# The last four input slabs of a hybrid mixer as plain float32 products

## The chip, the cores and the metric

The kernel runs on one core of one Trainium2 chip. The time is device microseconds (us) of one execution, and the measure is the median of several executions. The core has a matrix engine (TensorE, PE in the profile), a vector engine (VectorE, DVE), a scalar engine (ScalarE, ACT), GpSimd (POOL) and SyncE (SP), which here only issues the DMAs that fetch weights.

## The reference

The program is a stack of two small transformer blocks for 256 tokens of width 1024, all in float32. The stage that changes is the input projection of the "even mixer" of the second block:

```python
def even_mixer(h, w_in, w_out, dw_w, dw_b, ln_g, ln_b):
    proj = h @ w_in                                   # (256 x 1024) @ (1024 x 2560)
    q, k, v, u, gate = jnp.split(proj, [512, 1024, 1536, 2048], axis=-1)
    a_out = merge_heads(stick_breaking_attention(     # 8 heads of 64
        split_heads(q, 8), split_heads(k, 8), split_heads(v, 8)))
    c = u * jax.nn.sigmoid(gate)
    c = causal_depthwise_conv(c, dw_w, dw_b)          # 31 taps, 512 channels
    c = jax.nn.silu(layer_norm(c, ln_g, ln_b))
    return jnp.concatenate([a_out, c], axis=-1) @ w_out
```

## The kernel before

**Weights come in slabs.** A slab is 1 MB of a weight matrix (for the input projection 256 output columns), which SyncE's queue fetches into one of four slots `raw[0..3]`. ScalarE then writes the high part of each number to `w_hi` (`high_one`, L587), and VectorE (`low_one`, L1257) or GpSimd (`low_one`, L509) writes the rest, `raw - w_hi`, to `w_lo`. The activations are kept in the same way, in `x_hi` and `x_lo`, the two parts of `x_pair`. Both parts have the type float32r. The product of a slab is then three matmuls instead of one (`three`, L1906 to L1908): high by high, high by low, low by high.

```python
pe.matmul(out_ap, a_hi, b_hi, start=start, stop=False, skip_group_check=True)
pe.matmul(out_ap, a_hi, b_lo, start=False, stop=False, skip_group_check=True)
return pe.matmul(out_ap, a_lo, b_hi, start=False, stop=stop, skip_group_check=True)
```

A slot may be fetched anew when `slab_ready` has counted its low part, since from then on nobody reads `raw`.

**The stage.** The hybrid mixer has ten input slabs. Two wide ones give v; then come the list `HYB_IN`: slab 6 (u, half 0), 8 (gate, half 0), 0 (q, half 0), 2 (k, half 0), and then the four in question: 7 (u, half 1) in slot 0, 9 (gate, half 1) in slot 1, 1 (q, half 1) in slot 2, 3 (k, half 1) in slot 3. Each of these goes through `slab_into`, which makes 2 x 8 x 3 = 48 matmuls of 128 by 128 weights with 256 columns.

**The order is written out by hand on each engine.** TensorE puts the four slabs between the steps of the attention of heads 0 to 3:

```python
heads(stick_logits, 0); slab_into(4, 0)
heads(stick_logits, 1); slab_into(5, 1)
heads(stick_rest, 0);   slab_into(6, 2)
... wait: banks of slabs 0 and 1 are read out ...
heads(stick_values, 0); heads(stick_rest, 1); slab_into(7, 3)
```

`all_copied()` follows, which waits until ScalarE has read the last bank out (L617), then the logits of heads 4 to 7, warming matmuls on zeros (`keep_warm`, L2000), the rest of these heads, and `project_out`, the product with w_out. The logits of a head (L2388 to L2391), its `stick_rest` (L2399 to L2401) and its `stick_values` (L2410 to L2412) are matmuls of plain float32 already.

VectorE runs the depthwise convolution one tap at a time (`convolve(n)` is n taps, L1773). Between them stand its part of the attention, `bounds` (L1779) and `softplus` (L1787), the low parts of slabs, and `gated_half` (L1753), the product u x sigmoid(gate) that feeds half of the convolution. How many taps stand at each place is a constant.

## Time and profile before

| what | value |
|---|---|
| median of 3 runs | 1682.43 us (1682.34 to 1683.7) |
| the profiled execution | 1682.74 us |
| its span, first to last instruction | 1680.7 us |
| TensorE busy / weight loads | 97% / 84% of the span |
| VectorE busy | 71% |
| ScalarE busy | 51% |
| GpSimd busy | 7% |
| granted TensorE clock, mean | 0.997 of full speed |
| input projection of the hybrid mixer and its attention | from about 868 us to about 966 us |

The profiled execution is 2.04 us longer than its span, which is what lies around the first and the last instruction. A matmul's end is modelled in the profile, and matmuls overlap, so what one costs in a stream is read from the distance between two starts, not from its duration.

### The profile page before, as it was taken

Reading aid. Unit: us, or ns where it says so; the run is one execution under the profiler, and the core shown is the slowest. Engines: PE = TensorE matmul, PEld = TensorE weight load, DVE = VectorE, ACT = ScalarE, POOL = GpSimd, SP = SyncE. Lnnn points to the kernel's source line nnn. Section 1 sums busy time; section 2 is a strip of 40 time slices with the busy share of each in tenths; the row PEclk is TensorE's granted clock in tenths of the full one; section 3 lists DMA queues with packets and bytes.
Section 4 is the critical chain, followed back from the end, with each engine's and each line's share of the span. In section 5 each row is a group of like instructions: output and inputs, shape, how many; then the busy total and the mean of one; then the engine's idle time right before and its main releaser. Section 6 shows DMA issues by size and latency. Waiting matters only on the chain. (4 is left out here: it accounts for less than half of the span.)

```text
span 1680.7 us, 24860 instructions
## 1 busy us (share of the span) xinstructions
PE 1635.6 (97%) x9423; PEld 1415.3 (84%) x9432; DVE 1193.1 (71%) x1765; ACT 862.4 (51%) x1212; POOL 115.7 (7%) x36
## 2 busy tenths in 40 slices
PE   8999999989999999999999999999999999999998
PEld 7988888879788887888889778888888888888887
DVE  2896778777668788566679976667666675676665
ACT  6323655572665556544466373446544465364443
POOL 6351000012600000000010000000000000000000
PEclk9999999999999999999999999999999999999999
DMA  8623466755245556455644235555555653345552
GB/s 284 207 76 101 141 213 192 222 145 164 66 149 175 200 175 201 163 196 179 225 144 170 80 128 182 194 184 197 178 187 196 204 200 115 125 138 186 189 195 80
DMA packets 211035, 283.35 MB, mean 169 GB/s; under 512 B 13196, under 2 KB 179075, under 8 KB 210963
## 3 DMA queue, kind: packets, MB, share of 16 engines
q1 hardware_dynamic: 209475, 278.18, 50.4%
q10 hardware_dynamic: 1488, 4.17, 0.7%
q8 instruction: 50, 0.82, 0.2%
q14 instruction: 22, 0.18, 0.0%
HBM read 280.88 MB, written 1.44 MB: 168 GB/s over the span
## 5 line engine op out<-in xcount | busy, mean ns | idle before, releaser
L587 ACT ACTIVATE w_hi<-raw 128x2048 fp32r<-128x2048 f32 x257 | 488.5, 1908 | 169.0 <-PE ps L2082 88.1
L1335 DVE TENSOR_TENSOR w_lo<-raw,w_hi 128x2048 fp32r<-128x2048 f32 x162 | 371.1, 2291 | 192.3 <-ACT w_hi L587 192.3
L2078 PE MATMUL ps<-x_pair,w_hi 128*128 128x512 f32 x1664 | 415.2, 391 | 0.0
L2078 PEld LDWEIGHTS ps<-x_pair,w_hi 128*128 128x128 f32 x1664 | 302.6, 189 | 56.3
L2082 PEld LDWEIGHTS ps<-x_pair,w_lo 128*128 128x128 f32 x1664 | 227.0, 190 | 16.2
L2082 PE MATMUL ps<-x_pair,w_lo 128*128 128x256 f32 x1664 | 232.0, 282 | 0.0
L1906 PE MATMUL ps<-x_pair,w_hi 128*128 128x256 f32 (+1 forms) x704 | 200.9, 285 | 2.5 <-POOL w_lo L509 2.4
L1907 PE MATMUL ps<-x_pair,w_hi 128*128 128x256 f32 (+1 forms) x704 | 199.1, 283 | 0.0
L1908 PE MATMUL ps<-x_pair,w_lo 128*128 128x256 f32 (+1 forms) x704 | 199.1, 283 | 0.0
L1257 DVE TENSOR_TENSOR w_lo<-raw,w_hi 128x2048 fp32r<-128x2048 f32 x74 | 173.5, 2352 | 35.9 <-ACT w_hi L587 35.8
L1906 PE MATMUL ps<-w_hi,g_hi 128*128 128x512 f32 x480 | 187.5, 391 | 0.0
L1907 PE MATMUL ps<-w_lo,g_hi 128*128 128x512 f32 x480 | 187.5, 391 | 0.0
L1908 PE MATMUL ps<-w_hi,g_lo 128*128 128x512 f32 x480 | 186.7, 389 | 0.0
L1906 PE MATMUL ps<-w_hi,x_pair 128*128 128x512 f32 (+1 forms) x432 | 173.3, 401 | 9.4 <-DVE x_pair L1173 4.6
L1908 PE MATMUL ps<-w_hi,x_pair 128*128 128x512 f32 (+1 forms) x432 | 167.6, 388 | 0.0
L1907 PE MATMUL ps<-w_lo,x_pair 128*128 128x512 f32 (+1 forms) x432 | 167.3, 387 | 0.0
L509 POOL TENSOR_TENSOR w_lo<-raw,w_hi 128x2048 fp32r<-128x2048 f32 x21 | 99.6, 4769 | 730.5 <-ACT w_hi L587 730.5
L1362 DVE TENSOR_REDUCE arena<-ps 128x256 f32<-128x512 f32 x208 | 136.7, 684 | 9.1 <-PE ps L2082 6.6
L1906 PEld LDWEIGHTS ps<-x_pair,w_hi 128*128 128x128 f32 (+1 forms) x704 | 134.3, 191 | 6.1 <-POOL w_lo L509 3.4
L1907 PEld LDWEIGHTS ps<-x_pair,w_hi 128*128 128x128 f32 (+1 forms) x704 | 134.3, 191 | 0.7
L1908 PEld LDWEIGHTS ps<-x_pair,w_lo 128*128 128x128 f32 (+1 forms) x704 | 134.2, 191 | 0.2
L771 ACT ACTIVATE g_hi<-arena 128x256 fp32r<-128x256 f32 x120 | 44.0, 411 | 134.9 <-PE ps L1908 127.8
(184 smaller groups left out, 1817.1 us busy)
## 6 DMA issues: line engine op xcount, KB each, us to landing
raw<-in_ffn_w_in SPq DMA_DIRECT2D x80, 1024.0 KB, 5.1
raw<-in_ffn_w_out SPq DMA_DIRECT2D x44, 1024.0 KB, 4.9
raw<-in_ffn_w_up SPq DMA_DIRECT2D x40, 1024.0 KB, 5.1
raw<-in_ffn_w_down SPq DMA_DIRECT2D x22, 1024.0 KB, 5.0
raw<-in_hgrn_w_in SPq DMA_DIRECT2D x16, 1024.0 KB, 6.0
raw<-in_gla_w_in SPq DMA_DIRECT2D x12, 1024.0 KB, 5.3
raw<-in_hyb_w_in SPq DMA_DIRECT2D x10, 1024.0 KB, 5.6
raw<-in_ffn_w_in SPq DMA_DIRECT2D x16, 512.0 KB, 4.8
```

The lines of the kernel that those rows point to most:

```text
L509: pool.tensor_tensor(w_lo[slot][:, :], raw[slot][:, :], w_hi[slot][:, :].bitcast(F32), ALU.subtract)\
L587: act.activation(w_hi[slot][:, :], raw[slot][:, :], ACT.Copy).then_inc(hi_done[slot], 1)
L771: act.activation(dst[:, b, :], ff_g[:, b, :], ACT.Copy).then_inc(gt_hi[b], 1)
L1257: dve.tensor_tensor(w_lo[slot][:, :], raw[slot][:, :], w_hi[slot][:, :].bitcast(F32), ALU.subtract)\
L1335: dve.tensor_tensor(w_lo[slot][:, :], raw[slot][:, :], w_hi[slot][:, :].bitcast(F32), ALU.subtract)\
L1362: dve.tensor_reduce(ff_u[:, b, g, :], halves_of, AX_X, ALU.add).then_inc(part_sum[g][b], 1)
L1906: pe.matmul(out_ap, a_hi, b_hi, start=start, stop=False, skip_group_check=True)
L1907: pe.matmul(out_ap, a_hi, b_lo, start=False, stop=False, skip_group_check=True)
L1908: return pe.matmul(out_ap, a_lo, b_hi, start=False, stop=stop, skip_group_check=True)
L2078: pe.matmul(ps[:, bank, :], w_hi[s][:, at:at + P], x_pair[:, k, :, :].rearrange("p x t -> p (x t)"), start=k == 0, stop=False, skip_group_ ...
L2082: ins = pe.matmul(ps[:, bank, 0:SEQ], w_lo[s][:, at:at + P], x_hi[:, k, :], start=False, stop=k == NK - 1, skip_group_check=True)
```

## The change

The four slabs are no longer split. TensorE multiplies the raw float32 weights of the slot by whole float32 activations, one matmul where three stood. The whole activations are made once, by VectorE, as `x_hi + x_lo` into `xn`, whose old content is done with by then. The high and low parts of these four slabs drop out on ScalarE and VectorE. The taps that stood between the dropped low parts now stand together, and VectorE waits for the end of its memset ahead of the sum; nothing else of its list changes. Since the raw slot is now read by TensorE, the slabs of w_out that follow in the four slots are fetched when TensorE has used the slab (`slab_used`), and no longer when its low part is made.

```diff
-HYB_IN = ((2, 6), (3, 8), (2, 0), (3, 2), (0, 7), (1, 9), (2, 1), (3, 3))
+HYB_IN = ((2, 6), (3, 8), (2, 0), (3, 2))
+HYB_PLAIN = ((0, 7), (1, 9), (2, 1), (3, 3))
...
+        x_whole_sb = xn[:, :, :].rearrange("p b d -> p (b d)").rearrange("p (k t) -> p k t", t=SEQ)
...
+            def load_plain(slot, pieces):
+
+                load(slot, pieces)
+                plain_full[slot] = ring.dmas[slot]
+
+            def load_out_behind_plain(w, slots, order):
+
+                for s in order:
+                    u, _ = ring.take(s)
+                    sp.wait_ge(slab_used[s], u + 1)
+                    sp.sem_inc(slab_ready[s], 1)
+                    sp.dma_start(raw_rows(s), row_slab(w, slots.index(s) * SLAB)).then_inc(raw_full[s], 16)
...
-            load_out(hyb_out, HYB_OUT, HYB_OUT)
+            for s, col0 in HYB_PLAIN:
+                load_plain(s, [(raw_cols(s), col_slab(hyb_in, col0 * SLAB))])
+            load_out_behind_plain(hyb_out, HYB_OUT, HYB_OUT)
...
-                    high_one(0)
                     evacuate_pair((0, 1), hyb["v"], banks=(0, 1))
-                    high_one(1)
                     evacuate(2, words(0, 512), bank=6)
-                    high_one(2)
                     evacuate(3, words(1024, 512), 64 ** -0.5, bank=7)
-                    high_one(3)
...
                     low_one(3)
+                    dve.tensor_tensor(x_whole_sb, x_hi.bitcast(F32), x_lo.bitcast(F32), ALU.add).then_inc(x_whole, 1)
                     gated_half(0, 2, 3)
                     convolve(3)
                     low_one(3)
-                    convolve(2)
-                    low_one(0)
-                    low_one(1)
-                    convolve(9)
-                    low_one(2)
-                    convolve(7)
+                    convolve(18)
                     bounds(0)
-                    low_one(3)
                     convolve(6)
...
+                    def slab_plain(bank, s):
+
+                        pe.wait_ge(raw_full[s], plain_full[s])
+                        pe.wait_ge(proj_free[s], made[s] + 1)
+                        used[s] += 1
+                        made[s] += 1
+                        for b in range(2):
+                            for k in range(NK):
+                                at = k * SLAB + b * P
+                                ins = pe.matmul(ps[:, bank, b * SEQ:b * SEQ + SEQ], raw[s][:, at:at + P], x_whole_sb[:, k, :],
+                                                start=k == 0, stop=k == NK - 1, skip_group_check=True)
+                        ins.then_inc(slab_used[s], 1)
...
                     heads(stick_logits, 0)
-                    slab_into(4, 0)
+                    pe.wait_ge(x_whole, 1)
+                    slab_plain(4, 0)
                     heads(stick_logits, 1)
-                    slab_into(5, 1)
+                    slab_plain(5, 1)
                     heads(stick_rest, 0)
-                    slab_into(6, 2)
+                    slab_plain(6, 2)
```

What this does to the engines' orders is seen at three places. On TensorE, behind the logits of heads 0 and 1, the first of the four slabs begins before with the first of its 48 matmuls (`w_hi0` and `w_lo0` are the parts of slot 0):

```order
L2388 MATMUL ps<-arena 128x256
L2389 MATMUL ps<-arena 128x128
L2391 MATMUL ps<-const 128x128 x2
L1906 MATMUL ps<-x_pair,w_hi0 128x256 [waits proj_free0,slab_ready0]
L1907 MATMUL ps<-x_pair,w_hi0 128x256
L1908 MATMUL ps<-x_pair,w_lo0 128x256
```

The same place of the changed kernel (its lines stand some 25 further down), with the whole slab in two rows:

```order
L2413 MATMUL ps<-arena 128x256
L2414 MATMUL ps<-arena 128x128
L2416 MATMUL ps<-const 128x128 x2
L2403 MATMUL ps<-xn,raw0 128x256 [waits proj_free0,raw_full0,x_whole]
L2403 MATMUL ps<-xn,raw0 128x256 x15
L2413 MATMUL ps<-arena 128x256
```

So 16 matmuls with other operands stand for 48, between the same neighbours. On VectorE the piece from the low part of slab 8 (slot 3) to the taps behind `bounds(0)` is before:

```order
L1257 TENSOR_TENSOR w_lo3<-raw3,w_hi3 128x2048 [waits hi_done3]
L1773 SCALAR_TENSOR_TENSOR arena<-arena,cols 128x256 [waits cv_tap] x2
L1257 TENSOR_TENSOR w_lo0<-raw0,w_hi0 128x2048 [waits hi_done0]
L1257 TENSOR_TENSOR w_lo1<-raw1,w_hi1 128x2048 [waits hi_done1]
L1773 SCALAR_TENSOR_TENSOR arena<-arena,cols 128x256 [waits cv_tap] x9
L1257 TENSOR_TENSOR w_lo2<-raw2,w_hi2 128x2048 [waits hi_done2]
L1773 SCALAR_TENSOR_TENSOR arena<-arena,cols 128x256 [waits cv_tap] x7
L1779 TENSOR_SCALAR arena<-ps 128x384 [waits sb_z] x2
L1257 TENSOR_TENSOR w_lo3<-raw3,w_hi3 128x2048 [waits hi_done3]
L1773 SCALAR_TENSOR_TENSOR arena<-arena,cols 128x256 [waits cv_tap] x6
```

In the changed kernel, from the sum for the whole activations on:

```order
L1816 TENSOR_TENSOR xn<-x_pair 128x2048
L1770 TENSOR_TENSOR arena<-ps,arena 128x2x256 [waits proj_free3,slab_used2]
L1787 TENSOR_SCALAR arena<-arena,cols 128x256 [waits proj_free2]
L1787 TENSOR_SCALAR arena<-arena,cols 128x256
L1790 SCALAR_TENSOR_TENSOR arena<-arena,cols 128x256 [waits cv_tap]
L1274 TENSOR_TENSOR w_lo3<-raw3,w_hi3 128x2048 [waits hi_done3]
L1790 SCALAR_TENSOR_TENSOR arena<-arena,cols 128x256 [waits cv_tap] x18
L1796 TENSOR_SCALAR arena<-ps 128x384 [waits sb_z] x2
L1790 SCALAR_TENSOR_TENSOR arena<-arena,cols 128x256 [waits cv_tap] x6
```

Four low parts are gone, three of them ahead of the wait for the logits (`sb_z`), and the sum stands ahead of the first product u x sigmoid(gate). On SyncE's queue the fetches of w_out and what follows them are before:

```order
L386 DMA raw0<-in_hyb_w_out_2 128x2x1024 [waits slab_ready0]
L386 DMA raw1<-in_hyb_w_out_2 128x2x1024 [waits slab_ready1]
L386 DMA raw2<-in_hyb_w_out_2 128x2x1024 [waits slab_ready2]
L386 DMA raw3<-in_hyb_w_out_2 128x2x1024 [waits slab_ready3]
L386 DMA raw0<-in_ffn2_w_in_2 128x4x256 [waits slab_ready0]
```

and in the changed kernel:

```order
L411 DMA raw0<-in_hyb_w_out_2 128x2x1024 [waits slab_used0]
L411 DMA raw1<-in_hyb_w_out_2 128x2x1024 [waits slab_used1]
L411 DMA raw2<-in_hyb_w_out_2 128x2x1024 [waits slab_used2]
L411 DMA raw3<-in_hyb_w_out_2 128x2x1024 [waits slab_used3]
L390 DMA raw0<-in_ffn2_w_in_2 128x4x256 [waits slab_ready0]
```

The order is the same, and what the four fetches wait for has moved from VectorE's low parts to TensorE's use of the slabs; the fetches of the next FFN stand behind the last of them.

Of the kernel before, what the change touches and what calls it, by code (L numbers as in the profile page):

```python
# [26 lines left out]
P = 128  # L27
# [31 lines left out]
WARM_HEADS = 3  # L59
EACH = [slice(c, c + 1, 1) for c in range(NK)]  # L60
PAIRS = [slice(c, c + 2, 1) for c in range(0, NK, 2)]
HYB_IN = ((2, 6), (3, 8), (2, 0), (3, 2), (0, 7), (1, 9), (2, 1), (3, 3))
GLA_REST = (0, 1, 2, 3)
CROSS_BANK = {HG_HEADS: 4, GLA_HEADS: 5}
WIDE = 2 * SLAB
# [71 lines left out]
def build(nc, A, out):  # L137
    with ExitStack() as ctx:
# [3 lines left out]
        def sem(name):  # L142
            return ctx.enter_context(nc.semaphore(name))
# [85 lines left out]
        def col(name, i=0):  # L229
# [48 lines left out]
            sem("sb_z"), sem("sb_min"), sem("sb_ln"), sem("sb_sp"), sem("sb_rest"), sem("sb_w"), sem("sb_pv"))  # L278
        cv_tap, cv_turn, cv_ms, cv_std, cv_norm, cv_back, cv_silu = (
            sem("cv_tap"), sem("cv_turn"), sem("cv_ms"), sem("cv_std"), sem("cv_norm"), sem("cv_back"), sem("cv_silu"))  # L280
        stored = sem("stored")

        block = ctx.enter_context(nc.Block())

# [10 lines left out]
        def raw_rows(s):  # L295
            return raw[s][:, :].rearrange("p (c n) -> p c n", c=2)
# [60 lines left out]
        def sums_before(f):  # L357
            return f * (NF - 2) - min(f, 2)

        def halves(t, m):  # L360

            v = t.rearrange("p (n two m) -> p n two m", two=2, m=m)
            return v[:, :, 0, :], v[:, :, 1, :]
# [15 lines left out]
        def _(sp):  # L379
# [8 lines left out]
            def load_four_columns(w, c0, n):  # L388
                with sp.Fori(0, n) as i:
                    for s in range(RING):  # L390
                        sp.wait_ge(slab_ready[s], i + (ring.uses[s] + 1))
                        sp.dma_start(raw_cols(s), col_slab(w, i * (RING * SLAB) + (c0 + s * SLAB))).then_inc(raw_full[s], 16)
                for s in range(RING):
                    ring.skip(s, n)

            def load_four_wide(w, c0, n):
                with sp.Fori(0, n) as i:
# [11 lines left out]
            def load_out(w, slots, order):  # L409
                for s in order:  # L410
                    load(s, [(raw_rows(s), row_slab(w, slots.index(s) * SLAB))])  # L411
# [71 lines left out]
            load_wide_pair(hyb_in, 4 * SLAB, (0, 1))  # L483
            for s, col0 in HYB_IN:
                load(s, [(raw_cols(s), col_slab(hyb_in, col0 * SLAB))])
            load_out(hyb_out, HYB_OUT, HYB_OUT)
            load_ffn(3)
            load_ffn(4)
            load_wide_pair(gla_in, 4 * SLAB, (0, 1))
# [86 lines left out]
        def _(act):  # L576
# [12 lines left out]
            def high_one(slot, dmas=1):  # L589
                high(slot, *ring.take(slot, dmas))  # L590
# [401 lines left out]
            for l in range(2):  # L992
# [14 lines left out]
                if l == 0:  # L1007
# [23 lines left out]
                    high_one(2)  # L1031
                    sigmoid_gate(3, 0)
                    high_one(3)
                    high_one(0)
                    evacuate_pair((0, 1), hyb["v"], banks=(0, 1))
                    high_one(1)
                    evacuate(2, words(0, 512), bank=6)
                    high_one(2)
                    evacuate(3, words(1024, 512), 64 ** -0.5, bank=7)
                    high_one(3)  # L1040
                    softplus_logs(0)
                    softplus_logs(1)
                    made[0] += 1
# [75 lines left out]
        def _(dve):  # L1119
# [133 lines left out]
            def low_one(slot):  # L1253

                u, _ = lows.take(slot)
                dve.wait_ge(hi_done[slot], u + 1)
                dve.tensor_tensor(w_lo[slot][:, :], raw[slot][:, :], w_hi[slot][:, :].bitcast(F32), ALU.subtract)\  # L1257
                    .then_inc(slab_ready[slot], 1)
# [478 lines left out]
            for l in range(2):  # L1737
                ffn(False, 0, 2 + 2 * l)
                after_ffn(2 + 2 * l, ("norm_g_2", l * 6 + 2), True, 2 if l == 0 else None)
                if l == 0:  # L1740
                    hyb = hyb_views()
                    pad = CONV_TAPS - 1
                    dve.memset(hyb["pad"][:, :, 0:pad], 0.0)
                    lows.skip(2, 1)

                    def gated_half(half, u_slot, gate_slot):
# [49 lines left out]
                        stick_softplus(2 * pair + 1)  # L1796

                    low_one(3)
                    gated_half(0, 2, 3)
                    convolve(3)  # L1800
                    low_one(3)
                    convolve(2)
                    low_one(0)
                    low_one(1)
                    convolve(9)
                    low_one(2)
                    convolve(7)
                    bounds(0)
                    low_one(3)
                    convolve(6)  # L1810
                    softplus(0)
                    convolve(5)
# [87 lines left out]
        def _(pe):  # L1900
# [460 lines left out]
            for l in range(2):  # L2361
                turn_block(0)
                if l == 0:
# [15 lines left out]
                    slab_into(7, 3)  # L2379
                    all_copied()  # L2380

                    def stick_logits(hd):
                        a, c = hd % 2 * 64, hd // 2
                        q, k = hyb["q"][a:a + 64, c, :], hyb["k"][a:a + 64, c, :]
                        bank = ps[:, hd % 4, :]
                        if hd >= 4:
                            pe.wait_ge(sb_w, hd - 3)
                        pe.matmul(bank[:, 0:SEQ], k[:, 0:P], q, start=True, stop=False, skip_group_check=True)  # L2388
                        pe.matmul(bank[:, SEQ:SEQ + P], k[:, P:SEQ], q[:, P:SEQ], start=False, stop=False, skip_group_check=True)  # L2389
                        for c0 in (0, SEQ):  # L2390
                            ins = pe.matmul(bank[:, c0:c0 + P], ident, const[:, STRICT:STRICT + P], start=False, stop=False,  # L2391
                                            skip_group_check=True)
                        ins.then_inc(sb_z, 1)
# [31 lines left out]
                        step(2 * pair + 1)  # L2425

                    heads(stick_logits, 0)
                    slab_into(4, 0)
                    heads(stick_logits, 1)
                    slab_into(5, 1)  # L2430
                    heads(stick_rest, 0)
                    slab_into(6, 2)
                    for s in range(2):
                        pe.wait_ge(proj_free[s], made[s] + 1)
                    heads(stick_values, 0)
                    heads(stick_rest, 1)
                    slab_into(7, 3)
                    all_copied()
                    heads(stick_logits, 2)
                    heads(stick_logits, 3)  # L2440
# [74 lines left out]
```

## Rows read from the trace of the kernel before

**Rows 1.** Page, part 1: busy us (share of the span) and instructions.

```profile
PE 1635.6 (97%) x9423; PEld 1415.3 (84%) x9432; DVE 1193.1 (71%) x1765; ACT 862.4 (51%) x1212; POOL 115.7 (7%) x36
```

**Rows 2.** Windows of the stage: busy us of each engine, clock, DMA share, GB/s.

```profile
core 0: us, PE busy (x) PEld busy (x) DVE busy (x) ACT busy (x) POOL busy (x), PEclk, DMA share, GB/s
881.00:898.50 17.50, 17.05 (x121) 15.89 (x119) 16.02 (x22) 10.03 (x9) 1.02 (x1) 1.00 0.92 313
898.50:934.00 35.50, 33.83 (x260) 31.99 (x260) 34.25 (x71) 22.61 (x26) 0.00 (x0) 1.00 0.34 114
```

**Rows 3.** TensorE, in order of time: later waits. Columns: start, us, what, idle before.

```profile
934.36 0.67 PE L2388 MATMUL ps<-arena 64*128 64x256 f32 x2 [0.89 <-ACT arena L617]
...
945.83 0.70 PE L2399 MATMUL ps<-arena,const 128*128 128x256 f32 x2 [0.41 <-DVE arena L1787]
...
954.25 0.47 PE L1906 MATMUL ps<-w_hi,x_pair 128*128 128x512 f32 x1 [0.22 <-DVE x_pair L1561]
...
965.23 1.03 PE L2420 MATMUL ps<-const,arena 128*128 128x128 f32 x8
```

**Rows 4.** TensorE, in order of time: start and end of slot 2's slab.

```profile
917.83 0.36 PE L1906 MATMUL ps<-x_pair,w_hi 128*128 128x256 f32 x1
...
923.31 0.28 PE L1906 MATMUL ps<-x_pair,w_hi 128*128 128x256 f32 x1
923.43 0.28 PE L1907 MATMUL ps<-x_pair,w_hi 128*128 128x256 f32 x1
923.55 0.28 PE L1908 MATMUL ps<-x_pair,w_lo 128*128 128x256 f32 x1
924.63 0.43 PE L2410 MATMUL ps<-arena 128*64 128x128 f32 x2 [0.81 <-DVE arena L1753]
```

**Rows 5.** TensorE, in order of time: plain float32 with 256 columns.

```profile
917.03 0.60 PE L2399 MATMUL ps<-arena,const 128*128 128x256 f32 x2
917.47 0.38 PE L2400 MATMUL ps<-arena,const 128*128 128x128 f32 x2
...
1457.06 1.46 PE L2213 MATMUL ps<-arena 128*128 128x256 f32 x6
1458.36 0.59 PE L2000 MATMUL ps<-const 128*128 128x512 bf16 x2
```

**Rows 6.** Instructions of line 2399: durations in ns, first and last start.

```profile
L2399 PE MATMUL ps<-arena,const x16: 377/380/483, 916.2 to 948.8; 128*128 128x256 f32 x16
```

**Rows 7.** VectorE, in order of time, 871 to 940 us.

```profile
871.92 2.29 DVE L1257 TENSOR_TENSOR w_lo<-raw,w_hi 128x2048 fp32r<-128x2048 f32 x1 [1.06 <-ACT w_hi L587]
881.81 0.69 DVE L1753 TENSOR_TENSOR arena<-ps,arena 128x512 f32<-128x512 f32 x1 [7.59 <-ACT arena L617]
...
885.79 0.87 DVE L1773 SCALAR_TENSOR_TENSOR arena<-arena,cols 128x256 f32<-128x256 f32 x2
...
900.40 0.56 DVE L1779 TENSOR_SCALAR arena<-ps 128x384 f32<-128x384 f32 x1
901.88 0.56 DVE L1779 TENSOR_SCALAR arena<-ps 128x384 f32<-128x384 f32 x1 [0.93 <-PE ps L2391]
...
909.84 0.55 DVE L1779 TENSOR_SCALAR arena<-ps 128x384 f32<-128x384 f32 x1
910.61 0.56 DVE L1779 TENSOR_SCALAR arena<-ps 128x384 f32<-128x384 f32 x1 [0.21 <-PE ps L2391]
...
916.76 7.21 DVE L1773 SCALAR_TENSOR_TENSOR arena<-arena,cols 128x256 f32<-128x256 f32 x18
923.89 0.68 DVE L1753 TENSOR_TENSOR arena<-ps,arena 128x512 f32<-128x512 f32 x1
...
937.42 1.01 DVE L1779 TENSOR_SCALAR arena<-ps 128x384 f32<-128x384 f32 x2
```

**Rows 8.** ScalarE, in order of time, 923 to 934 us.

```profile
923.86 0.60 ACT L617 ACTIVATE arena<-ps 128x512 f32<-128x512 f32 x1 [1.12 <-PE ps L1908]
...
928.15 1.91 ACT L587 ACTIVATE w_hi<-raw 128x2048 fp32r<-128x2048 f32 x1
933.51 0.60 ACT L617 ACTIVATE arena<-ps 128x512 f32<-128x512 f32 x1 [3.45 <-PE ps L1908]
```

**Rows 9.** DMA issues, 868 to 982 us: count, KB, median us to landing.

```profile
raw<-in_hyb_w_in SPq DMA_DIRECT2D x5, 1024.0 KB, 7.7
raw<-in_hyb_w_out SPq DMA_DIRECT2D x4, 1024.0 KB, 5.3
```

More of the change, by code:

```diff
@@ L280, in build @@
             sem("cv_tap"), sem("cv_turn"), sem("cv_ms"), sem("cv_std"), sem("cv_norm"), sem("cv_back"), sem("cv_silu"))
-        stored = sem("stored")
+        stored, x_whole = sem("stored"), sem("x_whole")
+        plain_full = {}
         block = ctx.enter_context(nc.Block())
@@ L1033, in _ @@
                     high_one(3)
-                    high_one(0)
                     evacuate_pair((0, 1), hyb["v"], banks=(0, 1))
-                    high_one(1)
                     evacuate(2, words(0, 512), bank=6)
-                    high_one(2)
                     evacuate(3, words(1024, 512), 64 ** -0.5, bank=7)
-                    high_one(3)
+                    for s, _ in HYB_PLAIN:
+                        ring.take(s)
                     softplus_logs(0)
@@ L1742, in _ @@
                     pad = CONV_TAPS - 1
-                    dve.memset(hyb["pad"][:, :, 0:pad], 0.0)
+                    link(dve.memset(hyb["pad"][:, :, 0:pad], 0.0))
                     lows.skip(2, 1)
@@ L2436, in _ @@
                     heads(stick_rest, 1)
-                    slab_into(7, 3)
+                    slab_plain(7, 3)
                     all_copied()
```

## The prediction

> **What bounds the kernel now.** I read the page's busy times first: TensorE is busy 97% of the span, VectorE 71%, ScalarE 51% [rows 1]. That alone says that a saving on VectorE or ScalarE pays only where TensorE waits for them, and that each microsecond more on TensorE is likely to be paid in full. It has to be checked in the stage itself, so the second view is the windows. In the two windows that hold the four slabs and what leads to them TensorE is busy 17.05 of 17.50 us and 33.83 of 35.50 us, at full granted clock (1.00, that is 2.4 GHz), while VectorE has 16.02 and 34.25 us [rows 2]. The two are nearly level there, so neither share decides; the order of time must. I followed TensorE through the stage and noted every idle time with what ended it. There is 0.81 us ahead of the values of heads 0 and 1, ended by VectorE's `gated_half` (line 1753) [rows 4]; 0.89 us ahead of the logits of heads 4 to 7, ended by ScalarE's reading of the last slab's bank; 0.41 and 0.22 us ended by VectorE; and none ahead of the transposes of the finished convolution at 965.23 us [rows 3]. So TensorE is the chain through the stage. VectorE's 124 taps are done in time for those transposes, and only the waits named above hang on VectorE.
>
> **TensorE's part of the change.** Removed are 4 x 48 float32r matmuls, added are 4 x 16 plain float32 ones; all have 128 by 128 weights and 256 columns. A float32r matmul starts 0.12 us after the one before (923.31, 923.43, 923.55) [rows 4], so a slab takes 48 x 0.12 = 5.76 us. Counted from its first recorded start at 917.83 to one step behind the last, 923.67, it is 5.84 us [rows 4]; I keep the smaller one, since the first start is a modelled one, and take 5.84 for the low bound of the cost.
>
> A plain float32 matmul of this shape is in the trace twice over. Line 2399 runs once for each of 8 heads and has 16 records [rows 6]: each plain matmul is two records. From a start of its pair at 917.03 to the next line's at 917.47 are 0.44 us [rows 5]. Line 2213, the output of the linear attention, has other weights for each matmul, as the new slabs do, and six of its records start at 1457.06 with the next line's first at 1458.36: 1.30 / 6 = 0.217 us a record; by the group's length, (1.46 - 0.38) / 5 = 0.216, with 0.38 us for the last record [rows 5, 6]. A matmul is thus 0.43 us, a slab 16 x 0.432 = 6.91 us. Per (half, k) that is 0.432 where 3 x 0.12 = 0.36 stood. One for three is dearer, not cheaper.
>
> Four slabs: 4 x (6.91 - 5.76) = **+4.6 us** on TensorE. Bounds: +4.3 us with 5.84 for the old slab, +5.1 us with 0.44 for the new matmul (7.04).
>
> The Trainium skill's FP8 and Floating Point Precision, TensorE Precision Notes, says that true float32 is four passes through the array. The trace has two records for a matmul, each as long as two passes would be, so it agrees in the total work; if each of four passes cost a step as the old ones do, the slab would be 7.7 us and not 6.91. The sum goes by the two records.
>
> **What VectorE gives back.** Removed are four low parts of 2.29 us each, 9.2 us in all; added is one sum of the same 128 x 2048 elements, priced as a low part, 2.29 us [rows 7]. The sum stands where VectorE waits 7.59 us for the first sigmoid (until 881.81) [rows 7]: it ends by 876.6 us and costs nothing. Without that cover it would cost 2.3 us.
>
> Where do the 9.2 us go? Three of the four stand ahead of `bounds(0)`, which waits for the logits of heads 0 and 1. From 885.79 us on, 18 taps follow, at 7.21 / 18 = 0.40 us each, so VectorE is done at about 893, and the logits come as before: the first `bounds` instruction at about 900.4 us and the second at 901.88, which already waited for TensorE [rows 7]. 6.9 us of saved work become 7 us of waiting. The fourth low part stood behind `bounds(0)`: VectorE comes to `bounds(1)` at about 907.6 us instead of 909.84, but its second instruction waited for TensorE already (0.21 us, at 910.61) [rows 7], and that now comes 1.15 us later, behind one dearer slab: 911.75. So VectorE is back at TensorE's pace there, with nothing in hand. What is left is this: from there to the end of `gated_half`, 910.61 to 924.57, are 13.96 us of taps and softplus [rows 7], now 911.75 to 925.7, while TensorE comes to its wait for it after three dearer slabs at 923.67 + 3 x 1.15 = 927.1 us. The wait in [rows 4] is gone with 1.4 us in hand. It stretched from 923.67 to 924.63, 0.96 us; I take back 0.1 us for the step from one shape to another that stays: **-0.9 us**. Low bound of the gain 0, if something else ends last there; it cannot be more than 0.96.
>
> **ScalarE and the late fetches.** Four high parts (1.91 us each) go. Before they ran in gaps between readings of banks that waited for TensorE (1.12 and 3.45 us idle) [rows 8], so nothing comes of them. But the fetches of w_out now wait for TensorE's use. Slot 1's is issued at about 918.5 us and lands, at 5.3 us [rows 9], at 923.8; its high part is done at 925.7, before slot 2's bank is ready to read at 927.1. Slot 2's is issued at 927.1 and lands at 932.4; its high part stands on ScalarE ahead of the reading of slot 3's bank, for which TensorE waits: it ends at 934.3, and that bank is ready at 933.5 + 4.6 - 0.9 = about 937.2 us. 2.9 us in hand. With the 7.7 us that the crowded fetches of w_in took [rows 9], it would end at 936.7, still in time. On SyncE's queue the next FFN's fetches stand behind slot 3's and go out about 10 us later, near 937 instead of 927 us; nobody turns to them before the mixer's own product is done, past 965 us [rows 3]. Cost: 0.
>
> **Behind the four slabs.** The readout of the last bank, the logits of heads 4 to 7, VectorE's last `bounds`, the 11 taps and softplus, `stick_rest` and `project_out` all hang on TensorE's arrival and shift with it. VectorE's low part ahead of `bounds(2)` ended at 937.42 us while the first logits had been ready [rows 7]; now they come at about 939.3, and VectorE, at about 938.7, is there. It loses nothing and gains nothing.
>
> **Sum.** +4.6 - 0.9 = **+3.7 us**. The profiled execution took 1682.74 us (span 1680.7 and 2.04 around it), so 1686.4; it is 0.3 us above the median of 1682.43, against which I forecast **1686.1 us**. Bounds: 4.3 - 0.96 = +3.3, and 5.1 - 0 = +5.1, so 1685.7 to 1687.5.
>
> **Rivals.**
> 1. *Late fetches.* If slot 2's w_out takes more than 8.2 us to land, ScalarE holds the reading of slot 3's bank, and every microsecond beyond goes to TensorE. For it: the fetch, its high part and that bank's readout are now one row on the chain of one slab. Against it: 5.3 us median, and the queue is otherwise empty then. At a landing of 10 us it costs 1.8 us more: 1687.9. Chance 8%.
> 2. *Four steps a matmul.* The new stream has a weight load for each record, out of slots that DMA also fills, and might run at four steps of 0.12 us: 64 x 0.12 = 7.7 us on TensorE instead of 4.6, 1689.2 us. Against it: line 2213 has the same shape with fresh weights too. Chance 6%. The rule on four passes, above, would fit this one if each pass paid a full step.
> 3. *Faster.* It decides at one number: 5.76 / 32 = 0.18 us a record. If the two records of a plain matmul streamed in 0.12 us each here, a slab would be 3.84 us, TensorE would give up 1.92 us a slab, and from then on VectorE would set the pace: `gated_half` would end near 922.6 instead of 924.57 (its low part removed), the logits of heads 4 to 7 would begin 3.9 us earlier, and VectorE's `bounds` would let some 3.5 us through: 1678.9 us. Against it: 0.216 us in [rows 5]. Chance 6%, and 3% for a gain of another kind.
> 4. *No change that can be told.* Slack that I take for tied (0.89 us ahead of the logits, 0.41 ahead of `stick_rest`) absorbs part, or slabs behave more mildly: +0 to +3, about 1684. Chance 9%.
>
> **How the numbers follow.** Forecast as worked out 68%, rivals 8, 6, 9 and 9%. What a measurement of this kernel tells from no change is about 0.2%, 3.4 us, and my sum lies just past it: its own range, +3.3 to +5.1, reaches from 1685.7 to 1687.5, nearly all above 1685.8. With the runs' scatter I put 50 of the 68 to slower and 18 to no difference. Slower: 50 + 8 + 6 = 0.64; same: 18 + 9 = 0.27; faster 0.09. The range leaves out rival 3 and the far ends: 1683.2 to 1689.0.
>
> **What would show it.** Records of line 2403: 128 in all, 0.216 us apart, 6.9 us a slab. VectorE idle some 7 us ahead of `bounds(0)`. No idle time on TensorE ahead of the values of heads 0 and 1. The transposes of the convolution near 968.9 us instead of 965.23. Wrong would be another distance of records, or an idle time ahead of the logits of heads 4 to 7 above 0.9 us with ScalarE's high part in front of it.

## The result, and the profile after

| | median | executions | profiled execution: time, span |
|---|---|---|---|
| before | 1683.01 us | 20 (1680.67 to 1692.1) | 1682.74, 1680.7 us |
| changed | 1686.82 us | 20 (1684.45 to 1696.03) | 1686.17, 1684.2 us |

The ratio is 1.0022, with a 95% interval from 1.0011 to 1.0032: slower by 0.22%, +3.8 us between the medians and +3.5 us between the profiled spans. The forecast was +3.7. With 20 executions of each kernel the interval is about 1.8 us to either side, so a change of half this size would still have been told from none; the prediction had put that limit at 3.4 us.

The page after, part 1 (busy us, share of the span, instructions), answers to [rows 1]:

```profile
PE 1640.3 (97%) x9359; PEld 1416.0 (84%) x9368; DVE 1186.9 (70%) x1762; ACT 855.0 (51%) x1208; POOL 115.6 (7%) x36
```

VectorE lost 6.2 us of work and ScalarE 7.4, TensorE gained 4.7, and the kernel became slower by nearly what TensorE gained. The instructions of line 2403, the new matmuls (durations in ns, first and last start), and their order of time around slot 1's slab:

```profile
L2403 PE MATMUL ps<-xn,raw x128: 379/379/382, 901.5 to 936.7; 128*128 128x256 f32 x128
```

```profile
911.38 7.07 PE L2403 MATMUL ps<-xn,raw 128*128 128x256 f32 x32
918.29 0.59 PE L2424 MATMUL ps<-arena,const 128*128 128x256 f32 x2
```

There are 128 records for 64 matmuls, and the 32 of a slab, from 911.38 to the next line's start at 918.29, take 6.91 us, 0.216 us each, where 5.76 stood. This is the distance read from line 2213 in [rows 5], to the last digit.

TensorE's order of time after, at the places of [rows 3] and [rows 4]:

```profile
925.66 1.46 PE L2403 MATMUL ps<-xn,raw 128*128 128x256 f32 x6
927.05 0.43 PE L2435 MATMUL ps<-arena 128*64 128x128 f32 x2
...
937.95 0.67 PE L2413 MATMUL ps<-arena 64*128 64x256 f32 x2 [0.89 <-ACT arena L636]
...
949.41 0.70 PE L2424 MATMUL ps<-arena,const 128*128 128x256 f32 x2 [0.40 <-DVE arena L1804]
...
957.82 0.47 PE L1918 MATMUL ps<-w_hi,x_pair 128*128 128x512 f32 x1 [0.21 <-DVE x_pair L1578]
...
968.81 1.03 PE L2445 MATMUL ps<-const,arena 128*128 128x128 f32 x8
```

The idle time ahead of the values of heads 0 and 1 is gone (the row at 927.05 has none). The three others kept their size, 0.89, 0.40 and 0.21 us against 0.89, 0.41 and 0.22, although all around them moved by more than 3 us, so they absorbed nothing. The transposes begin 3.58 us later than in [rows 3], in a stage that was entered 0.19 us earlier.

VectorE after, which answers to [rows 7]:

```profile
874.02 2.29 DVE L1816 TENSOR_TENSOR xn<-x_pair 128x2048 f32<-128x2048 f32 x1
881.63 0.69 DVE L1770 TENSOR_TENSOR arena<-ps,arena 128x512 f32<-128x512 f32 x1 [5.32 <-ACT arena L636]
...
885.60 7.21 DVE L1790 SCALAR_TENSOR_TENSOR arena<-arena,cols 128x256 f32<-128x256 f32 x18
900.21 0.56 DVE L1796 TENSOR_SCALAR arena<-ps 128x384 f32<-128x384 f32 x1 [7.40 <-PE ps L2416]
...
911.59 0.56 DVE L1796 TENSOR_SCALAR arena<-ps 128x384 f32<-128x384 f32 x1 [0.93 <-PE ps L2416]
...
924.86 0.68 DVE L1770 TENSOR_TENSOR arena<-ps,arena 128x512 f32<-128x512 f32 x1
...
939.51 0.56 DVE L1796 TENSOR_SCALAR arena<-ps 128x384 f32<-128x384 f32 x1 [1.06 <-PE ps L2416]
```

The sum of the two parts costs 2.29 us inside the wait, which shrank from 7.59 to 5.32. The three dropped low parts turned into 7.40 us of waiting for the logits. And `gated_half` begins at 924.86, 0.97 us *later* than the 923.89 of before, with a whole low part less ahead of it. At `bounds(2)`, the last row, VectorE waits 1.06 us for the logits of heads 4 to 7.

ScalarE and the fetches that now wait for TensorE:

```profile
923.54 1.91 ACT L606 ACTIVATE w_hi<-raw 128x2048 fp32r<-128x2048 f32 x1 [0.47 <-DMA raw<-in_hyb_w_out]
927.16 0.60 ACT L636 ACTIVATE arena<-ps 128x512 f32<-128x512 f32 x1 [1.71 <-PE ps L2403]
...
932.38 1.91 ACT L606 ACTIVATE w_hi<-raw 128x2048 fp32r<-128x2048 f32 x1 [1.70 <-DMA raw<-in_hyb_w_out]
937.09 0.60 ACT L636 ACTIVATE arena<-ps 128x512 f32<-128x512 f32 x1 [2.81 <-PE ps L2403]
```

Two high parts now wait for their DMA, but both are done before the bank that ScalarE must read next is ready: after the second it still waits 2.81 us for TensorE. The forecast was 2.9 us in hand.

### The profile page after: what moved, and what is told of

Its sections match the earlier page's. It is cut to its first block and busy times, and to the rows that moved or that the text cites. A ratio compares the mean times of both kernels' runs of the same rounds, so it can differ in the third digit from the quotient of the medians.

```text
span 1684.2 us, 24750 instructions
## 1 busy us (share of the span) xinstructions
PE 1640.3 (97%) x9359; PEld 1416.0 (84%) x9368; DVE 1186.9 (70%) x1762; ACT 855.0 (51%) x1208; POOL 115.6 (7%) x36
## 5 line engine op out<-in xcount | busy, mean ns | idle before, releaser
L606 ACT ACTIVATE w_hi<-raw 128x2048 fp32r<-128x2048 f32 x253 | 480.9, 1908 | 170.9 <-PE ps L2094 88.1
L1352 DVE TENSOR_TENSOR w_lo<-raw,w_hi 128x2048 fp32r<-128x2048 f32 x162 | 371.1, 2291 | 192.6 <-ACT w_hi L606 192.6
L1274 DVE TENSOR_TENSOR w_lo<-raw,w_hi 128x2048 fp32r<-128x2048 f32 x70 | 164.5, 2359 | 35.4 <-ACT w_hi L606 35.3
L1918 PE MATMUL ps<-x_pair,w_hi 128*128 128x256 f32 (+1 forms) x640 | 182.4, 285 | 2.5 <-POOL w_lo L528 2.4
L1920 PE MATMUL ps<-x_pair,w_lo 128*128 128x256 f32 (+1 forms) x640 | 181.0, 283 | 0.0
L1919 PE MATMUL ps<-x_pair,w_hi 128*128 128x256 f32 (+1 forms) x640 | 181.0, 283 | 0.0
L1918 PEld LDWEIGHTS ps<-x_pair,w_hi 128*128 128x128 f32 (+1 forms) x640 | 122.0, 191 | 5.8 <-POOL w_lo L528 3.1
L1919 PEld LDWEIGHTS ps<-x_pair,w_hi 128*128 128x128 f32 (+1 forms) x640 | 121.9, 190 | 0.7
L1920 PEld LDWEIGHTS ps<-x_pair,w_lo 128*128 128x128 f32 (+1 forms) x640 | 121.9, 190 | 0.2
```

Source lines behind the costliest of these rows:

```text
L606: act.activation(w_hi[slot][:, :], raw[slot][:, :], ACT.Copy).then_inc(hi_done[slot], 1)
L1274: dve.tensor_tensor(w_lo[slot][:, :], raw[slot][:, :], w_hi[slot][:, :].bitcast(F32), ALU.subtract)\
L1352: dve.tensor_tensor(w_lo[slot][:, :], raw[slot][:, :], w_hi[slot][:, :].bitcast(F32), ALU.subtract)\
```

## The experiments

Each experiment ran beside the kernel before on the same chip, and time differences are between these medians, with the ratio and its 95% interval behind. The runs e1 to e4, e5 to e8, and e9 and e10 were made on three different chips, on which the kernel before had medians of 1683.04, 1682.82 and 1683.48 us, so a comparison across these groups is the weaker one.

**e1: VectorE's saving alone.** The kernel before, with the four low parts cut to a few columns; `low_none` stands where `low_one` stood for the four slabs.

```diff
+                dve.tensor_tensor(w_lo[slot][:, 0:8], raw[slot][:, 0:8], w_hi[slot][:, 0:8].bitcast(F32), ALU.subtract)\
+                    .then_inc(slab_ready[slot], 1)
```

> The kernel before, with VectorE's low parts of the four slabs cut to 8 of 2048 columns (so their w_lo is mostly stale: the low parts of these four slabs are left out of the result). TensorE runs its 48 matmuls a slab as before. It prices alone what the change gives back on VectorE, 9.2 us of work. Theory 1 (TensorE's arrivals set the pace; three of the parts stand ahead of the logits and the fourth ahead of a second wait for logits at 910.61 us): nothing comes of it, 0 to -0.1 us, and the 0.96 us gap ahead of the values of heads 0 and 1 stays. Theory 2 (the prediction's words: the gap goes because VectorE has less to do): -0.9 us and the gap is gone. Theory 3 (VectorE is as much the bound as TensorE): -3 us or more.

Measured: 1683.01 us against 1683.04, ratio 1.0001 (0.9986 to 1.0017). TensorE's gap is where it was:

```profile
923.57 0.28 PE L1915 MATMUL ps<-x_pair,w_lo 128*128 128x256 f32 x1
924.65 0.43 PE L2417 MATMUL ps<-arena 128*64 128x128 f32 x2 [0.80 <-DVE arena L1760]
```

The interval, -2.4 to +2.9 us, doesn't exclude the -0.9 of theory 2; the trace decides. Besides the gap, the transposes of the convolution begin at 965.26 us, before at 965.23. 9 us less work on VectorE are worth nothing, and do not close the gap either. That is theory 1, and against the heading under which the prediction booked the 0.9 us.

**e2: TensorE's side alone.** The changed kernel with the parts put back as dead work; w_out's fetch waits for the low part and for TensorE.

```diff
-                    sp.wait_ge(slab_used[s], u + 1)
-                    sp.sem_inc(slab_ready[s], 1)
+                    sp.wait_ge(slab_ready[s], u + 1)
+                    sp.wait_ge(slab_used[s], u + 1)
...
-                    convolve(18)
+                    convolve(2)
+                    low_one(0)
+                    low_one(1)
+                    convolve(9)
+                    low_one(2)
+                    convolve(7)
                     bounds(0)
+                    low_one(3)
```

(and the four `high_one` on ScalarE).

> The changed kernel, with all four high parts on ScalarE and all four low parts on VectorE put back where they stood; nobody reads them, TensorE multiplies raw weights. It prices TensorE's side alone. Theory 1: the gap ahead of the values of heads 0 and 1 goes because TensorE comes later, not because VectorE comes earlier, so the whole is +3.7 us over the kernel before, the same as the change itself. Theory 2: +4.6 us, since nothing is given back. Theory 3: more than +4.6.

Measured: 1687.06 us against 1683.04, +4.0, ratio 1.0023 (1.0012 to 1.0033); the change itself has 1.0022. Theory 1 forecast +3.7 and theory 2 +4.6, which the interval of the ratio does not tell apart; the trace does:

```profile
925.15 2.11 PE L2411 MATMUL ps<-xn,raw 128*128 128x256 f32 x9
927.18 0.43 PE L2443 MATMUL ps<-arena 128*64 128x128 f32 x2
```

```profile
925.00 0.68 DVE L1772 TENSOR_TENSOR arena<-ps,arena 128x512 f32<-128x512 f32 x1
```

The gap has closed with all four low parts in place, and `gated_half`, the VectorE row, is 1.1 us later than before and still done 1.5 us ahead of TensorE. The gap closed because TensorE arrives 3.5 us later (927.18 instead of 923.67, of which 0.96 us had been idle), not because VectorE arrives earlier.

**e3: half of the new matmuls.** `for k in range(0, NK, 2)` in `slab_plain`.

> The changed kernel with only every second of the 16 plain matmuls of each of the four slabs (half of the products' sums over k is left out of the result). A slab costs TensorE 3.46 us, less than the 5.76 before. It tests the threshold at which VectorE takes over. Worked out on the trace of before: logits of heads 4 to 7 begin 4.5 us earlier than in the kernel before, but VectorE, whose gated_half ends near 922 us, lets 3.6 us through: -3.6 us against before, about -7.3 against the change. If TensorE alone set the pace (no limit by VectorE) it would be 4 x -2.3 - 1 = -10 us against before. If the change's cost had nothing to do with the length of the slabs, it would stay near +3.8.

Measured: 1684.85 us against 1683.04, from 1679.9 to 1691.7 in 11 runs, ratio 1.0002 (0.9987 to 1.0016). All three figures of the expectation missed. The windows of its profile point to the clock (columns: stretch, us, TensorE busy, granted clock, DMA share, GB/s):

```profile
924.00:926.00 2.00, 0.25 (x2) 1.00 0.38 33
926.00:928.00 2.00, 0.00 (x0) 1.00 0.95 367
928.00:930.00 2.00, 0.36 (x2) 0.63 0.31 125
930.00:932.00 2.00, 2.00 (x13) 0.50 0.00 0
```

```profile
929.64 0.69 PE L2435 MATMUL ps<-arena 128*64 128x128 f32 x2 [5.39 <-DVE arena L1770]
```

TensorE came 5.4 us too early for `gated_half`, stood idle, and its clock fell from 2.4 to 1.2 GHz (0.50) for what followed, and a second time from about 942 to 952 us. The other executions fit this: the four near 1680 us have a mean granted clock of 0.995 or 0.996, the four from 1684.9 to 1685.5 us one of 0.989 to 0.991.

The profiled execution was the slowest of the eleven, and most of what it has above the others was lost far ahead of the edit. One low part on VectorE, at 70.92 us, takes 6.67 us; the same one takes 2.28 us in the kernel before. TensorE then waits 4.90 us, up to 80.13 us, where the kernel before is busy all through, its clock is at half from about 79 to 89 us, and VectorE's first `gated_half` begins at 889.12 instead of 881.81 us:

```profile
70.92 6.67 DVE L1274 TENSOR_TENSOR w_lo<-raw,w_hi 128x2048 fp32r<-128x2048 f32 x1
...
80.13 3.64 PE L2210 MATMUL ps<-arena 128*128 128x64 f32 x16 [4.90 <-DVE arena L1540]
...
889.12 0.69 DVE L1770 TENSOR_TENSOR arena<-ps,arena 128x512 f32<-128x512 f32 x1 [5.34 <-ACT arena L636]
...
974.23 1.03 PE L2445 MATMUL ps<-const,arena 128*128 128x128 f32 x8
```

From that `gated_half` to the transposes it took 85.1 us, against 83.4 in the kernel before: +1.7 us, as the medians have it.

**e4: VectorE's freed time put to use.** The changed kernel in another order. More taps stand ahead of the first `bounds` calls, and the convolution's transposes and normalisation move ahead of and under the first half of `project_out`:

```diff
-                    convolve(18)
+                    convolve(35)
                     bounds(0)
...
-                    convolve(5)
+                    convolve(10)
                     bounds(1)
-                    convolve(12)
+                    convolve(8)
                     softplus(1)
+                    low_one(0)
...
-                    bounds(2)
-                    bounds(3)
-                    convolve(11)
+                    for hd in range(4, 8):
+                        stick_bound(hd)
+                        convolve(2 if hd < 7 else 6)
...
-                    keep_warm(18)
+                    keep_warm(9)
...
-                    keep_warm(8)
+                    conv_turned()
+                    keep_warm(4, 0)
...
-                    project_out(HYB_OUT, lambda tb, k: base + k // 2 + 1, ks=range(4))
-                    conv_turned()
-                    keep_warm(16, 4)
-                    pe.wait_ge(cv_norm, NTB)
+                    project_out(HYB_OUT, lambda tb, k: base + k // 2 + 1, {(1, 0): turn_normed}, ks=range(4))
```

(`turn_normed` is that wait and the transposes behind it; the 8 warming matmuls after them are gone too. ScalarE's high part of slot 0 moves ahead of the second sigmoid.)

> The changed kernel with VectorE's freed time put to use: 17 more taps ahead of the first bounds (where it sits idle 7.4 us), 5 more behind them, two taps between the bounds of heads 4 to 7, the transposes of the convolution ahead of the first half of project_out and its normalisation hidden behind that half, so that 24 of the warming matmuls in between go, and 9 of the 18 ahead of stick_rest. Theory 1: the 9.2 us of VectorE are worth nothing only because its order leaves them idle; here TensorE loses 5.3 us of warming at the end and 2.0 to 2.6 us ahead of stick_rest: -7 to -8 us against the change, -3 to -4.5 against the kernel before. If taps still end too late for the transposes (past 954 us), it is less, and TensorE waits there. If the clock falls for want of warming, it shows as PEclk under 1.00 and +3 us or more.

Measured: 1679.04 us against 1683.04, -4.0, ratio 0.9975 (0.9965 to 0.9986), -7.8 against the change's median: as theory 1 had it. But the 11 times fall into two groups, five at 1676.3 to 1677.5 and five at 1679.0 to 1680.5, and one at 1684.8. The profiled execution has the clock at half for some 10 us:

```profile
936.00:938.00 2.00, 1.20 (x6) 1.00 0.00 0
938.00:940.00 2.00, 1.91 (x10) 1.00 0.82 201
940.00:942.00 2.00, 2.00 (x9) 0.60 1.01 394
942.00:944.00 2.00, 2.00 (x8) 0.50 1.09 378
```

It begins some 3 us behind the 0.89 us gap ahead of the logits of heads 4 to 7. Behind the other gap, of 0.78 us ahead of the logits of heads 0 and 1, the clock was at half for about 3.5 us.

**e5: the end of the same order on the kernel before.** The end of e4's diff (from `bounds(2)` on) on the split slabs. The 17 taps ahead of the first `bounds` stay where they were: with split slabs VectorE comes to it at 900.40 us without idle time [rows 7], so there is no room for them.

> The kernel before (its four slabs still split into parts), with the same end as e4: bounds of heads 4 to 7 with two taps between, 9 warming matmuls less ahead of stick_rest, convolution transposes ahead of project_out, normalisation hidden behind its first half, the 24 warming matmuls there gone. It asks whether e4's gain is the reordering's alone. Theory 1: VectorE has no free time here, so its 124 taps end at about 958 to 960 us, some 7 us after TensorE comes to the transposes; TensorE stands there, and what is won behind is lost again: -1 to +3 us against the kernel before, and e4 stays ahead of it by 3 us or more. If the reordering alone were worth it, this kernel would be 7 us faster than before.

Measured: 1685.16 us against 1682.82, +2.3, ratio 1.0011 (0.9999 to 1.0023), within theory 1's range. Ten of the 11 runs lie between 1683.5 and 1685.9 us; one, at 1731.99 us with a mean granted clock of 0.905, is left out of the ratio. TensorE waits for the last tap:

```profile
960.80 1.97 PE L2419 MATMUL ps<-const,arena 128*128 128x128 f32 x8 [8.48 <-DVE arena L1773]
```

The eight transposes took 1.97 us instead of 1.03, since the clock had fallen during that wait (0.50). So a part of e5's time is the clock; e9 takes that away.

**e6: e4 with TensorE's two gaps filled.**

```diff
                     slab_into(7, 3)
+                    pe.wait_ge(proj_free[0], made[0] + 1)
+                    keep_warm(4, 0)
                     all_copied()
...
                     slab_plain(7, 3)
+                    keep_warm(4, 0)
                     all_copied()
```

> e4 with four warming matmuls in each of TensorE's two gaps ahead of logits (heads 0 and 1, heads 4 to 7), where it waits 0.8 to 0.9 us for a bank's readout. In e4's profile the granted clock fell to 0.50 right behind both gaps, for about 5 and 10 us, and its times fall into 1676.3 to 1677.5 and 1679.0 to 1680.5. Theory 4 (the gaps let the clock fall in some executions): the upper group goes, the profile has 1.00 all through the stage, and the median is 1677, -6 us against the kernel before. If the fall has nothing to do with the gaps: as e4, 1679 in the median, with 0.50 behind them again.

Measured: 1677.08 us against 1682.82, **-5.7**, ratio 0.9961 (0.9947 to 0.9976). All 11 times lie between 1675.7 and 1677.7; the upper group is gone, and the same windows read:

```profile
940.00:942.00 2.00, 2.00 (x11) 1.00 1.00 399
942.00:944.00 2.00, 2.00 (x13) 1.00 1.08 377
```

The transposes of the convolution now begin at 954.68 us, and the last taps are just in time for them:

```profile
954.68 1.09 PE L2447 MATMUL ps<-const,arena 128*128 128x128 f32 x8 [0.17 <-DVE arena L1790]
```

This is the best version of the study and beats both kernels. Its times are those of e4's lower group; what each of its parts is worth, the earlier taps, the moved transposes and the dropped warming, was not measured alone.

**e7: the changed kernel with the two gaps filled**, the same two lines.

> The changed kernel with the same four plus four warming matmuls in the two gaps ahead of logits and nothing else. Of its 20 runs 13 lie between 1684.5 and 1687.0, six between 1688.6 and 1689.9. Theory 4: the upper group is executions in which the clock fell behind a gap; it goes, and the median is 1686, between 0 and -1 us against the change, +3 against the kernel before. Otherwise the six in twenty stay.

Measured: 1686.62 us against 1682.82, +3.8, ratio 1.0021 (1.001 to 1.0033). The times between 1688.6 and 1689.9 are gone (1684.5 to 1687.8 in 11 runs), but the median is where it was. (e2, with the gaps unfilled, has only one of 11 above 1688.6, so their absence is weak evidence by itself.) The +3.8 us of the change are not a matter of the clock.

**e8: e3 with the clock kept**, by the same two lines and `keep_warm(20)` behind `slab_plain(6, 2)`.

> e3 (half of the four slabs' products left out) with the same warming in the two gaps, and 20 warming matmuls more where TensorE waited 5 us for VectorE's gated_half and the clock fell to 0.50 behind it. Theory 1 with the clock kept: what e3 was to show, -3.6 us against the kernel before, VectorE being the limit. If it is still near 0, the limit of VectorE lies higher than worked out.

Measured: 1678.62 us against 1682.82, -4.2, ratio 0.9975 (0.9958 to 0.9992). In us the interval is -7.1 to -1.3, and the -3.6 that was worked out lies inside. The trace gives the size more sharply: from the first `gated_half` to the transposes are 79.6 us, before 83.4, so -3.8. VectorE is the limit, as TensorE's wait for `gated_half` and VectorE's unbroken run through all four bounds show:

```profile
920.86 0.43 PE L2437 MATMUL ps<-arena 128*64 128x128 f32 x2 [1.07 <-DVE arena L1770]
```

```profile
880.27 0.69 DVE L1770 TENSOR_TENSOR arena<-ps,arena 128x512 f32<-128x512 f32 x1 [5.34 <-ACT arena L636]
...
933.64 1.95 DVE L1796 TENSOR_SCALAR arena<-ps 128x384 f32<-128x384 f32 x4
...
959.86 1.03 PE L2447 MATMUL ps<-const,arena 128*128 128x128 f32 x8
```

**e9: the end of e6's order and its warming, with split slabs**, that is e5 with both gaps filled and 34 warming matmuls ahead of `conv_turned()`.

> e5 with TensorE kept busy where it stood: four warming matmuls in each of the two gaps ahead of logits as in e6, and 34 in the 8.5 us in which it waits for VectorE's last taps (in e5 the clock fell to 0.50 behind that wait). It is e6 with the four slabs split into parts, so it tells what plain slabs are worth in this order. Theory 1: the taps still end at about 960.5 us, the transposes stand there and not at 954, so 0 to +2 us against the kernel before, and 5 to 8 us behind e6. If clock and order alone made e6, this kernel is near 1677 too.

Measured: 1682.59 us in 6 runs against 1683.48 in 11, ratio 1.0001 (0.9974 to 1.0028). The transposes wait for the last tap although nothing else is in their way:

```profile
951.23 7.51 PE L1999 MATMUL ps<-const 128*128 128x512 bf16 x34
959.78 1.09 PE L2421 MATMUL ps<-const,arena 128*128 128x128 f32 x8 [1.03 <-DVE arena L1773]
```

Two of the 6 runs lie at 1690.2 and 1691.0 us, two of the 11 at 1691.4 and 1692.9. The transposes begin at 959.78 us, 5.1 us behind e6's 954.68, and TensorE spends 7.5 us before them on zeros. e6 is 5.7 us faster than the kernel before by its medians, this one 0.9 us, within its noise (the interval is -4.4 to +4.7 us; 0 to +2 was expected). Between the two medians, on two chips, are 5.5 us, where 5 to 8 were expected. The end of the order and the warming alone are worth nothing that can be told; they need the taps early. That no other order of the split slabs could gain is not shown.

**e10: the kernel before with the two gaps filled.**

> The kernel before with the four plus four warming matmuls in the two gaps ahead of logits and nothing else: what they are worth by themselves. Theory 4: the clock fell there in few executions of the kernel before (3 of 33 near 1691), so the median stays within 0.5 us of it.

Measured: 1682.76 us in 6 runs against 1683.48 in 11, ratio 0.9998 (0.9972 to 1.0024): no difference that can be told. One of the 6 runs is at 1692.19 us, with both gaps filled, so the executions near 1692 us do not come from these gaps alone.

## Why the prediction was right, step by step

- **TensorE's price, +4.6 us.** Right: 0.216 us a record, 6.91 us a slab in the trace, as in [rows 5]. One plain float32 matmul costs 0.432 us and replaces three that cost 0.36.
- **The total, +3.7 us.** The trace has 3.58 us and 0.19 for the earlier start, 3.77 in all, so the sum is right for its reasons. That the medians also differ by just 3.8 is luck in its last digits, with an interval of 1.8 us to either side. The time itself was forecast as 1686.1 and came out as 1686.82 us; 0.6 us of that is the median of the kernel before, 1682.43 us in 3 runs and 1683.01 in 20.
- **The 0.9 us back.** Right in size, wrong in its heading. The prediction booked it under what VectorE gives back. e1 gives VectorE's whole saving and keeps the gap; e2 gives none of it and closes the gap. It comes back because TensorE pays: `gated_half` moves late by one dearer slab (0.97 us in the trace), TensorE's arrival by three, and 0.96 us of the difference were idle. The prediction's own times (925.7 against 927.1 us) said so already; its words did not. So of the 9.2 us removed on VectorE nothing arrived in the kernel's time, not 0.9.
- **Where the low parts went.** Right: 7.40 us of waiting ahead of `bounds(0)`, forecast 7.
- **The sum x_hi + x_lo at nothing.** Right: 2.29 us inside a wait of 7.59.
- **The late fetches at nothing.** Right: 2.81 us in hand, forecast 2.9. How much later they could come before they cost anything was not tried.
- **Everything behind shifts.** Right: the three waits kept their sizes, and the transposes came at 968.81 us, forecast 968.9. VectorE was at `bounds(2)` at 938.45 us and the logits came at 939.51, forecast 938.7 and 939.3.
- **Rivals.** Four steps a matmul and two records at 0.12 us are both out by the trace. That small waits are slack that absorbs part is out too: they kept their sizes. That VectorE sets the pace once slabs are cheap, as the faster rival has it, e8 shows at one point: at 3.46 us a slab 3.8 us come through in the trace (4.2 between the medians) where 3.6 was worked out, while TensorE's own saving would have been about 10. At which cost of a slab it takes over was not measured. The clock, which e3 ran into first, was in none of the rivals.

## What to carry to other kernels

Count a change of matmul type in the distance between two starts and in records, not in instructions: one plain float32 matmul is two records of 0.216 us here, and so loses to three float32r matmuls of 0.12. Work taken from an engine that waits for another by a written order only lengthens its wait; it becomes time when the order is changed with it, so that what the bottleneck fills with warming can be dropped (e6 against e7: -9.5 us between their medians, with the same slabs; the earlier taps, the moved transposes and the dropped warming came together). And test an order on both variants: the one that gave 5.7 us with plain slabs gave, as far as it fits them, nothing that can be told with split ones (e9). Where a profiled execution is an outlier, compare the stage in it, from one event to another, before its whole time: e3's was 6.9 us above its median, and 7.3 us had been lost before it reached the stage.

## What the runs showed of the hardware

- **A gap of less than a microsecond goes with a fallen clock in some executions.** In e4's profile the granted clock was 0.50 (1.2 GHz) for some 10 us, beginning about 3 us behind a gap of 0.89 us, while TensorE was busy with the short matmuls of the logits. Half of e4's times lay 2 to 3 us above the others, and four warming matmuls in each of two such gaps removed that group (e6, none of 11). In the changed kernel 6 of 20 times lay 2 to 3 us above the others, all six with a mean granted clock of 0.995 where the 13 below have 0.996 to 0.999; none of e7's 11 lies there. No such execution of the changed kernel was profiled, so that its clock fell behind the gaps is argued and not shown. Filling them took about 2 us off e4's median and nothing off that of the changed kernel or of the kernel before. The same gaps stand in the profiles of the kernel before and of the change, at a full clock. What else sets whether it falls, the runs do not show.
- **The clock also falls elsewhere in the program.** The granted clock is under 1.00 in stretches of several us that no experiment touches: around 680 to 688 us in the profiles of the kernel before and of the change, 360 to 376 us in those of e7 and e10, 79 to 89 us in e3's, which then reached the stage 7.3 us late. The profiles of e4 and e8 have 1.00 in these three places and reach the first `gated_half` 1.5 to 1.7 us earlier than that of the kernel before (880.12 and 880.27 against 881.81). The times near 1692 us, 3 of the kernel before's 20, are as far above the rest; they stay with both gaps filled (one of 6 in e10). None of them was profiled, so whether a VectorE instruction that takes 4.4 us longer than its like, as in e3, is behind them stays open. One such instruction is in every profile that was looked at, at about 378 us, between 4.5 and 6.6 us long; why it takes that long is open too.
- **A longer wait costs more than itself.** 5.4 us idle in e3 were followed by about 6 us at half clock, and another 10 us followed later; with that wait and the two gaps filled (e8) the way from the first `gated_half` to the transposes took 79.6 instead of 85.1 us, and the median went from 1684.85 to 1678.62, without shortening any work.
- **The Trainium skill's FP8 and Floating Point Precision, TensorE Precision Notes**, has true float32 as four passes through the array. The trace agrees in amount: two records of 0.216 us, together 0.432 us. As an estimate from e9's row, 34 bf16 matmuls of 512 columns take 7.51 us, the last of them some 0.38 us as recorded; that is 0.216 us from start to start and 0.108 us for 256 columns, and four of these, if a bf16 matmul is one pass, are 0.432 us. They show as two records, not four.
